# A Mamba-2, latent-attention and neighbourhood-attention stack: the decay exponents computed on VectorE instead of ScalarE, and the per-head order of the output products

## The reference, cut to what matters

```python
xbc = silu(causal_depthwise_conv(xbc, conv_w, conv_b))       # x, B, C of the group
dt = softplus(dt + dt_bias); a = -exp(a_log)
a_cs = cumsum(dt * a)                                         # one row per head, decreasing
decay[l, s] = exp(a_cs[l] - a_cs[s])   if l >= s else 0
cb[l, s]    = sum_n C[l, n] * B[s, n]
y[l, j]     = sum_s (cb * decay)[l, s] * dt[s] * x[s, j] + d_skip * x[l, j]
g = rms_norm(y * silu(z)) * norm_g                            # per group of 256 channels
h = h + g @ w_out
```

## Time and profile before

| | us |
|---|---|
| runs of the kernel before | 1216.34, 1216.22, 1207.99 (median 1216.22) |
| the profiled execution, whole | 1216.34 |
| its span, first to last instruction | 1214.6 |
| PE busy | 1156.4 (95%) |
| DVE busy | 755.0 (62%) |
| ACT busy | 675.5 (56%) |
| POOL busy | 185.4 (15%) |

### The profile page before, as it was taken

How to read it: one execution, slowest core, us unless ns; L and a number is a source line. 1 busy time by engine, 2 the same in 40 slices (tenths; PEclk the granted TensorE clock), 3 DMA queues, 4 the chain that set the end, 5 groups by cost and what they waited for, 6 DMA issues and landing times.

```text
span 1214.6 us, 23737 instructions
## 1 busy us (share of the span) xinstructions
PE 1156.4 (95%) x8898; PEld 1093.9 (90%) x8898; DVE 755.0 (62%) x1123; ACT 675.5 (56%) x1071; POOL 185.4 (15%) x134
## 2 busy tenths in 40 slices
PE   6999999999999999679898999999999999999998
PEld 5988988899999999556668999999998999999998
DVE  4788778668665554536646666555677578666543
ACT  4788878655554343457725555444544565555332
POOL 0443453317000001022302000000000211000000
PEclk8999999999999999779979999999999999999999
DMA  5544344485555554322204555555544455555553
GB/s 195 183 163 157 124 155 158 123 246 169 173 173 174 177 171 134 104 80 94 70 18 139 188 179 187 190 178 185 174 139 135 142 177 189 180 185 189 190 178 100
DMA packets 53225, 190.32 MB, mean 157 GB/s; under 512 B 5920, under 2 KB 7072, under 8 KB 53168
## 3 DMA queue, kind: packets, MB, share of 16 engines
q1 hardware_dynamic: 51408, 182.95, 45.8%
q0 software_dynamic: 1760, 6.59, 1.7%
HBM read 188.44 MB, written 1.08 MB: 156 GB/s over the span
## 4 chain that ended last, share of the span: by engine, by line
PE 80%; issue 8%; DVE 6%; ACT 3%; POOL 2%; DMA 0%; POOLq 0%; DVEq 0%; ACTq 0%; SPq 0%
PE lin L412 24%; PE lin L414 23%; PE lin L413 23%; DVE w_lo L1205 2%; POOL y L1761 1%; POOL w_lo L1743 1%; PE lin L641 1%; ACT w_hi L824 1%; PE ps L682 1%; PE ps L683 1%; PE lin L639 1%; PE ps L756 1%; PE ps L779 1%; DVE cv L1284 1%; PE ps L445 1%
## 5 line engine op out<-in xcount | busy, mean ns | idle before, releaser
L1205 DVE TENSOR_TENSOR w_lo<-w_raw,w_hi 128x1024 fp32r<-128x1024 f32 x303 | 381.4, 1261 | 278.0 <-ACT w_hi L824 278.0
L824 ACT ACTIVATE w_hi<-w_raw 128x1024 fp32r<-128x1024 f32 (+2 forms) x343 | 354.7, 1040 | 254.2 <-PE lin L414 250.6
L412 PE MATMUL lin<-x_hi,w_hi 128*128 128x256 f32 (+1 forms) x1528 | 445.4, 291 | 10.9 <-DVE x_lo L1231 3.7
L414 PE MATMUL lin<-x_hi,w_lo 128*128 128x256 f32 (+1 forms) x1528 | 439.0, 287 | 0.0
L413 PE MATMUL lin<-x_lo,w_hi 128*128 128x256 f32 (+1 forms) x1528 | 438.2, 287 | 0.0
L412 PEld LDWEIGHTS lin<-x_hi,w_hi 128*128 128x128 f32 x1528 | 292.0, 191 | 15.1 <-DVE x_lo L1231 4.1
L413 PEld LDWEIGHTS lin<-x_lo,w_hi 128*128 128x128 f32 x1528 | 291.5, 191 | 1.5 <-issue 1.0
L414 PEld LDWEIGHTS lin<-x_hi,w_lo 128*128 128x128 f32 x1528 | 292.3, 191 | 0.0
L414 PE MATMUL lin<-hid_hi,w_lo 128*128 128x256 f32 (+1 forms) x768 | 218.2, 284 | 0.0
L413 PE MATMUL lin<-hid_lo,w_hi 128*128 128x256 f32 (+1 forms) x768 | 217.9, 284 | 0.0
L412 PE MATMUL lin<-hid_hi,w_hi 128*128 128x256 f32 (+1 forms) x768 | 217.4, 283 | 0.0
(11 more groups left out here) (252 smaller groups left out, 1527.4 us busy)
## 6 DMA issues: line engine op xcount, KB each, us to landing
w_raw<-w SPq DMA_DIRECT2D x343, 512.0 KB, 3.3
acs_bc<-acs_dram POOLq DMA_DIRECT2D x8, 544.0 KB, 4.8
bias_mask<-rpb POOLq DMA_DIRECT2D x4, 512.0 KB, 9.8
h<-h SPq DMA_DIRECT2D x4, 272.0 KB, 4.3
out<-h SPq DMA_DIRECT2D x8, 128.0 KB, 3.1
cst<-const SPq DMA_DIRECT2D x1, 784.0 KB, 9.1
vecs<-vec SPq DMA_DIRECT2D x1, 131.5 KB, 2.2
acs_dram<-y POOLq DMA_DIRECT2D x1, 34.0 KB, 2.4
```

The costliest lines, as they stand in the source:

```text
L412: mm3(o, wh, xh, start=first and i == 0, stop=False)
L414: ins = mm3(o, wl, xh, start=False, stop=last and i == kts - 1)
L824: a(w_hi[pg.slot][:, 0:n], w_raw[pg.slot][:, 0:n], ACT.Copy).then_inc(w_hi_done, pages)
L1205: tt(w_lo[pg.slot][:, 0:n], w_raw[pg.slot][:, 0:n], w_hi[pg.slot][:, 0:n].bitcast(F32), ALU.subtract)\
```

## The change

`decay_logs` on ScalarE is taken out (12 activations a group) and `log_decays` on VectorE put in (12 `tensor_scalar` instructions a group), both halves of group s-1 in slot s, behind the `silu` for B and C and ahead of `g_low`. It computes `min(acs_bc + (-cols), 0)`, so `cols` is now stored with its sign turned for the three columns concerned, and the exponential of `decay` loses its scale of -1. Its wait for `acs_in` and `ee_done` moves with it. In `y_products` the loop over the heads is now outside: each head runs its 272, 144 and 16 columns in a row, and then the other head does; the wait on `mm_done` stands in the loop with the same value for both heads. One start-up wait counts three memsets instead of four.

```diff
-                    pe.wait_ge(mm_done, g.times(2, q + 1).value)
-                    halves = [(slice(e * HD, (e + 1) * HD), 2 * q + e) for e in range(2)]
-                    for rows, j in halves:
-                        nc.tensor.matmul(o[rows, 0:T], x_tok[:, 0, j * HD:(j + 1) * HD], mm[:, j, 0:T],
-                                         start=True, stop=False)
-                    for rows, j in halves:
-                        nc.tensor.matmul(o[rows, 128:T], x_tok[:, 1, j * HD:(j + 1) * HD], mm[:, j, T:416],
-                                         start=False, stop=False)
-                    for rows, j in halves:
-                        ins = nc.tensor.matmul(o[rows, 256:T], x_tok[0:META, 2, j * HD:(j + 1) * HD],
-                                               mm[0:META, j, 416:432], start=False, stop=True)
+                    for e in range(2):
+                        j = 2 * q + e
+                        pe.wait_ge(mm_done, g.times(2, q + 1).value)
+                        rows = slice(e * HD, (e + 1) * HD)
+                        cs = slice(j * HD, (j + 1) * HD)
+                        nc.tensor.matmul(o[rows, 0:T], x_tok[:, 0, cs], mm[:, j, 0:T], start=True, stop=False)
+                        nc.tensor.matmul(o[rows, 128:T], x_tok[:, 1, cs], mm[:, j, T:416], start=False, stop=False)
+                        ins = nc.tensor.matmul(o[rows, 256:T], x_tok[0:META, 2, cs], mm[0:META, j, 416:432],
+                                               start=False, stop=True)
                     ins.then_inc(y_done, 1)
...
-            def decay_logs(g, half):
-
-                if half == 0:
-                    act.wait_ge(acs_in, (g + 1).times(16).value)
-                    if g.base == 0:
-                        act.wait_ge(cols_done, 4)
-                    else:
-                        act.wait_ge(ee_done, g.times(2).value)
-                for j in (2 * half, 2 * half + 1):
-                    h_at = g.times(4, j)
-                    for s, (rows, at, n, l0) in enumerate(((P, 0, T, 0), (P, T, 144, 128), (META, 416, 16, 256))):
-                        ins = a(dd[0:rows, j, at:at + n], acs_bc[0:rows, j, l0:T], ACT.Relu, scale=-1.0,
-                                bias=cols[0:rows, 3 + s, bass.ds(h_at.value, 1)])
-                ins.then_inc(dd_done, 1)
...
-                a(ee[:, hs, :], dd[:, hs, :], ACT.Exp, scale=-1.0).then_inc(ee_done, 1)
+                a(ee[:, hs, :], dd[:, hs, :], ACT.Exp).then_inc(ee_done, 1)
...
-                if has_lin and s.base:
-                    decay_logs(s, 0)
...
-                    if not s.base:
-                        decay_logs(s, 0)
-                    decay_logs(s, 1)
...
-                for i in (0, 3):
-                    nc.vector.tensor_copy(cols[:, i:i + 2, :], src[:, i:i + 2, :]).then_inc(cols_done, 1)
-                    nc.vector.tensor_copy(cols[0:META, i + 2, :], src[0:META, i + 2, :]).then_inc(cols_done, 1)
+                for i, sign in ((0, 1.0), (3, -1.0)):
+                    ts(cols[:, i:i + 2, :], src[:, i:i + 2, :], sign, None, ALU.mult).then_inc(cols_done, 1)
+                    ts(cols[0:META, i + 2, :], src[0:META, i + 2, :], sign, None, ALU.mult).then_inc(cols_done, 1)
...
+            def log_decays(g, half):
+
+                if half == 0:
+                    dve.wait_ge(acs_in, (g + 1).times(16).value)
+                    if g.base:
+                        dve.wait_ge(ee_done, g.times(2).value)
+                for j in (2 * half, 2 * half + 1):
+                    h_at = g.times(4, j)
+                    for s, (rows, at, n, l0) in enumerate(((P, 0, T, 0), (P, T, 144, 128), (META, 416, 16, 256))):
+                        ins = ts(dd[0:rows, j, at:at + n], acs_bc[0:rows, j, l0:T],
+                                 cols[0:rows, 3 + s, bass.ds(h_at.value, 1)], 0.0, ALU.add, ALU.min)
+                ins.then_inc(dd_done, 1)
...
                     silu(g, 1, bc_s[:, :, :], cv[:, 2:4, :], sg[:, 2:4, :])
+                    log_decays(g, 0)
+                    log_decays(g, 1)
```

More of the change, by code:

```diff
@@ L852, in _ @@
             act.wait_ge(vec_in, 16)
-            act.wait_ge(memset_done, 4)
+            act.wait_ge(memset_done, 3)
             for kt in range(KD):
@@ L1222, in _ @@
             dve.memset(dd[:, :, 416:432], 0.0)
-            dve.memset(cbm[:, 416:432], 0.0).then_inc(memset_done, 1)
+            dve.memset(cbm[:, 416:432], 0.0)
             dve.wait_ge(vec_in, 16)
```

## The result

The changed kernel takes 1221.99 us (median; 1217.81 to 1225.16), the kernel before 1216.34 us (1207.99 to 1218.71). The ratio on record is 1.0061, 95% interval 1.0037 to 1.0086 (the quotient of these two medians is 1.0046): slower by 0.5 to 0.6%, inside the range of the forecast and 3 us under it. The profiled execution spans 1220.0 us, 5.4 more than before.

A forecast was written before the change was run, and what follows sets the result against it. The DVE, ACT and POOL loop sets 25.0 us a slot; afterwards PE's 24.05 + 2.0 = 26.05 binds. Six slots +6.2, half slot +2.0, end +0.5 make +8.7 on 1216.34: 1225 us, range 1212 to 1231.

The forecast's parts named there:

- the PE loop: PE's cycle through a slot, between starts of two y_products: 24.05 us before, 26.05 after, becoming the longest loop.
- The half slot: Half slot leading to the last group also carries the product of group 6: +2.0 us.
- the last y_products: It lengthens PE before its wait for the output gate, so part is absorbed: +0.5 us.
- Part 1: Exponents leave ACT, POOL's y2 ends earlier, the second loop falls from 25.0 to at most 24.0: alone worth 5.8 us.
- Part 2: Exponents come to DVE: 2.6 us taken (1.9 to 3.7), plus up to 2.35 of POOL hold; costed at nothing.
- That hides the middle value: DVE's 5.5 us of idle time in a slot covers the exponents and POOL's hold; cost nothing.
- the first rival: In y_products the new order costs the old 2.15 us, only the exponents' gain remains: 1210.5 us, chance 0.12.
- Part 3: New order of y_products on PE: four heads cost 3.8 to 4.2 us against 2.15; 2.0 more taken.
- the row with the same pattern: Latent attention, one head at a time on the same rows: scaled, 1.06 us a head, 4.2 for four.
- heads overlap anyway: Rival for y_products: both array halves still run together, costing 0; 1210.5 us, chance 0.12.
- DVE becomes the bound: Rival: 3.7 us of exponents plus full POOL hold, 0.6 to 1 us a slot more, 1229 to 1231; chance 0.12.
- The clock did not fall: Rival: clock falls in slots that no longer absorb it, about 1.8 us each; two give 1229; chance 0.11.

The follow-up runs named there:

- page_first: Kernel before, with ACT's rounding of a slot's last page put ahead of the second half of the decay exponents: 1207.13 us, ratio 0.9921.
- order_alone: Kernel before with only the new order of y_products, decay exponents staying on ACT: 1224.47 us, ratio 1.0057.
- full_rows: Changed kernel, one head after the other, with each head's last block run over all 128 rows (zeros in rows 16 to 127): 1218.63 us, ratio 1.001.
- exponents_alone: Changed kernel with the old order of y_products, exponents staying on DVE: 1218.32 us, ratio 1.0004 to the kernel before.
- order_page_first: Kernel before with the new order of y_products and ACT's page rounding ahead of the second half of the exponents: 1224.05 us, ratio 1.0043.
- short_split: exponents_alone with POOL's third page split of a slot cut from 1024 to 16 columns: 1203.72 us, ratio 0.9897 to the kernel before.
- tails_paired: Changed kernel with only the 16-row blocks of two heads side by side again: 1219.18 us, ratio 1.0011 to the kernel before.

## Why the prediction was right

**The loops.** The forecast rested on the PE loop becoming the longest: 24.05 + 2.0 = 26.05 us a slot. It measured 25.84, made of a term for y_products that was 0.1 too small (2.09) and a chain from the end of chunk 0 to line 492 that was 0.3 too long (8.74 instead of 9.04: 126.19 to 134.93 in the trace of the changed kernel). The 0.3 lay in the one slot that the sum was read from. DVE's first convolution instruction starts 129.29 - 128.21 = 1.08 us behind ACT's first tap there. In the slot of 23.74 us of the same trace it is 0.71 (lines below), and in the changed kernel 130.25 - 129.53 = 0.72:

```profile
129.29 2.53 DVE L1284 SCALAR_TENSOR_TENSOR cv<-lin,vecs,cv 128x271 f32<-128x271 f32 x6 [3.22 <-ACT cv L894]
...
203.65 1.03 ACT L894 ACTIVATE cv<-lin,vecs 128x272 f32<-128x272 f32 x2
...
204.36 2.59 DVE L1284 SCALAR_TENSOR_TENSOR cv<-lin,vecs,cv 128x271 f32<-128x271 f32 x6 [2.88 <-ACT cv L894]
```

So the PE loop was 23.74, the shortest length in the earlier trace rows, and 23.74 + 2.09 = 25.83 is what was measured. Why one slot is 0.3 longer is open; it is the third of the six, as in page_first (24.06) and order_alone (26.16). (The longest of the six slots is also not the 26.36 that the prediction names but one that it doesn't show, 26.49.) Six slots cost 155.1 - 150.1 = 5 instead of 6.2 us. The half slot grew by 2.09 as forecast, and the last y_products left 0.9 us at the first matmul of the next stage. The first y_products started 1.6 us earlier in the profiled run, which the sum didn't have. That is the execution and not the edit: the mean granted clock up to there is 0.95 against 0.92 in the profile of before, and two experiments start as that one does (order_alone 65.35 us, full_rows 65.75, both at 0.92) while all others start at 62.98 to 64.72 at 0.95. Without it the profiles differ by +8.0 at the end of the phase, of the forecast 8.7; with it by +6.4, and the medians by +5.7. How much of the 3 us between forecast and median is chance of this kind is open.

**Part 1** was priced at 5.8 us, as gone from ACT alone. Page_first shows it at 10 us (0.79%, interval 0.5 to 1.1%). In the profiles 7.1 us of it are in the six slots, which fall to a PE loop of 23.74 instead of 24.05 and have no fall of the clock; the start adds 2.5 us, mostly the better start of that execution. The place was right: POOL's start, not ACT's busy time. In the change it is worth nothing, for both reasons, each shown by a run: the PE loop hides it (order_page_first), and DVE eats it (exponents_alone).

**Part 2** is where a step failed. "That hides the middle value; I cost it at nothing" is true in the changed kernel, with 0.99 us to spare, but only since a longer slot makes room. The sizes were good: 2.45 us for the 12 instructions against the 2.6 that it took, and 3.3 for the hold against up to 3.75. (The expectations of exponents_alone and short_split went by 2.0 and came out low for it: 3.4 us forecast, 3.72 measured.) The prediction then took 1.4 of that hold off, as already paid in DVE's own split today, and set the rest against all idle time of the slot. The critical stretch is shorter than the slot: it begins when ACT's sigmoid is done and ends at the taps. Counted there, the exponents make a loop of 25.0 by themselves, and part 1 plus part 2 together leave the time as it was (ratio 1.0004), not the gain of 5.8 us that the sum and the first rival both assumed. The forecast of the whole was unharmed since it never used them on the longest loop.

**Part 3.** The price was right (2.09 against 2.0), and so was the choice of the row with the same pattern, over the products of a full array. The mechanism was wrong. It is not that heads must be neighbours: they run together across a distance of four records. What parts them is the 16-row block between two heads, with the 0.20 us of the earlier trace rows. The prediction's rule gave the right price because such a block stands at every seam of the changed kernel. The page of the Trainium skill that the prediction put beside it (TensorEngine Tiling (Array Packing), Key Properties) has both halves of this: a change of tiling mode drains the engine, and different tiles run in parallel. tails_paired and full_rows agree with both. The prediction took the first for a detail of the seam.

**The rivals.** That heads overlap anyway is refuted in this kernel. Its price of 1210.5 also was wrong: with the y_products cost at zero (exponents_alone) the time is that of before, since DVE binds. That DVE becomes the bound was given 0.12; it holds as soon as y_products is cheap. The clock did not fall in the changed kernel's full slots (1.00 in each), where no stall is above 0.96 us; the order of y_products takes away the stalls of 1.94 us and more that stood before the falls.

## What to carry over

When two loops of almost equal length run through a stage, a change is priced by the longest loop after it, and each part has to be tried against every loop: here one part cost its full price and the other, measured alone, was worth nothing. Idle time of an engine is not room for new work unless it lies between the event that lets the work start and the one that waits for it. Before work is moved off an engine to free it, look at the order on that engine: exchanging two statements gave 0.8%, and a second exchange brought it to 1.6%.

## What the runs showed of the hardware

- DVE's `tensor_scalar` on fp32 in SBUF and POOL's `tensor_tensor` exclude each other instruction by instruction: one DVE instruction of the twelve took 2.43 us beside a POOL instruction of 2.45, against a median of 0.28. The twelve together need 2.45 us without a hold and 5.79 with it. The stretch shrinks by what POOL's instruction shrinks (2.13 for 2.2 us).
- TensorE runs fp32 matmuls of the two column halves at the same time also when others of the first half stand between them in the program, up to four records away here, and can start ahead of them. A block with 16 rows between them stops that: the heads start 1.06 us apart with it and 0.51 without (4.24 and 2.47 us a group).
- Filling 16 rows up to 128 with zeros made the block cheaper: a group of y_products fell from 2.15 to 1.75 us with heads alternating, and from 4.24 to 2.47 with one head after the other.
- The granted clock fell to its lower level (1.2 instead of 2.4 GHz) at the end of PE stalls of 1.94 to 2.99 us or within 1 us behind them, in five of seven such stalls in the profiles of before and of exponents_alone, and not once in the full slots of the changed kernel, of page_first, of full_rows and of short_split, whose stalls are 0.8 to 1.8 us.
